# Norm sums in columns of tokens, and filler products, around the first feed-forward tiles

## The reference

```
z  = merged @ w_out
x1 = x + z * rsqrt(mean(z*z) + eps) * g_post          # first norm
h2 = x1 * rsqrt(mean(x1*x1) + eps) * g_mlp            # second norm
f  = square(relu(h2 @ w_ff1)) @ w_ff2
```

## Time and profile before

| | |
|---|---|
| median of 3 runs | 2012.83 us (2011.98 to 2015.08) |
| the profiled execution | 2014.58 us, its span 2012.8 us |
| mean granted clock of TensorE | 0.989 of full speed |
| PE busy | 1957.8 us |
| DVE, ACT, POOL busy | 903.7, 621.5, 896.5 us |

### The profile page before, as it was taken

How to read it: one execution, slowest core, us unless ns; L and a number is a source line. 1 busy time by engine, 2 the same in 40 slices (tenths; PEclk the granted TensorE clock), 3 DMA queues, 4 the chain that set the end, 5 groups by cost and what they waited for, 6 DMA issues and landing times.

```text
span 2012.8 us, 33480 instructions
## 1 busy us (share of the span) xinstructions
PE 1957.8 (97%) x13077; PEld 1908.2 (95%) x13077; DVE 903.7 (45%) x1966; ACT 621.5 (31%) x1184; POOL 896.5 (45%) x533
## 2 busy tenths in 40 slices
PE   8999999999999999999989999799999999999996
PEld 6999999999999999999969999699999999999996
DVE  6504550154403552054577743888676740111126
ACT  6312211122012220122146546644444453212121
POOL 7453233333333233423442237579777764443412
PEclk9999999999999999999999999899999999999999
DMA  5312331134211331123654354513323252223412
GB/s 190 105 43 85 136 110 43 43 115 141 74 53 58 136 136 43 43 89 141 225 175 147 123 158 129 137 46 124 124 88 125 77 211 87 103 85 105 147 53 85
DMA packets 89289, 218.22 MB, mean 108 GB/s; under 512 B 7721, under 2 KB 40745, under 8 KB 88793
## 3 DMA queue, kind: packets, MB, share of 16 engines
q1 hardware_dynamic: 78784, 192.48, 28.6%
q10 hardware_dynamic: 10392, 24.14, 3.4%
HBM read 162.93 MB, written 53.66 MB: 108 GB/s over the span
## 4 chain that ended last, share of the span: by engine, by line
PE 88%; DVE 5%; issue 2%; ACT 2%; POOL 2%; DMA 0%; DVEq 0%; SPq 0%; ACTq 0%; POOLq 0%
PE bank L892 78%; PE bank L1041 1%; PE bank L1044 1%; PE bank L1235 1%; PE bank L1033 1%; PE bank L996 1%; PE bank L1039 1%; PE bank L1133 1%; POOL w_lo L698 1%; DMA w_raw<-w_stream 0%; ACT P_sb L1437 0%; POOL h_lo L713 0%; DVE acc L2074 0%; DVE gates L2071 0%; DVE acc L1763 0%
## 5 line engine op out<-in xcount | busy, mean ns | idle before, releaser
L892 PE MATMUL bank<-h_hi,w_hi 128*128 128x344 f32 (+1 forms) x2048 | 651.1, 318 | 2.4 <-POOL w_lo L698 2.2
L892 PE MATMUL bank<-h_lo,w_hi 128*128 128x344 f32 (+1 forms) x2048 | 637.7, 311 | 0.0
L892 PE MATMUL bank<-h_hi,w_lo 128*128 128x344 f32 (+1 forms) x2048 | 636.0, 311 | 0.0
L702 POOL TENSOR_TENSOR w_hi<-w_raw,ones 128x1024 fp32r<-128x1024 f32 x77 | 147.4, 1914 | 628.1 <-PE bank L892 628.1
L892 PEld LDWEIGHTS bank<-h_hi,w_hi 128*128 128x128 f32 x2048 | 387.4, 189 | 7.1 <-issue 3.5
L892 PEld LDWEIGHTS bank<-h_hi,w_lo 128*128 128x128 f32 x2048 | 387.2, 189 | 0.9
L892 PEld LDWEIGHTS bank<-h_lo,w_hi 128*128 128x128 f32 x2048 | 387.1, 189 | 0.0
L704 POOL TENSOR_TENSOR w_lo<-w_raw,w_hi 128x1024 fp32r<-128x1024 f32 x77 | 185.7, 2412 | 6.1
L2241 DVE TENSOR_TENSOR acc<-acc,bank 128x344 f32<-128x344 f32 x72 | 36.9, 513 | 292.0 <-PE bank L892 292.0
L1268 ACT ACTIVATE side_t<-bank 128x344 f32<-128x344 f32 x96 | 44.0, 459 | 284.3 <-PE bank L892 284.3
L1763 DVE SCALAR_TENSOR_TENSOR acc<-acc,rstd 128x258 f32<-128x258 f32 x128 | 126.7, 1032 | 0.1
(11 more groups left out here) (434 smaller groups left out, 4407.7 us busy)
## 6 DMA issues: line engine op xcount, KB each, us to landing
w_raw<-w_stream SPq DMA_DIRECT2D x113, 512.0 KB, 3.7
d_side<-side_t ACTq DMA_DIRECT2D x32, 516.0 KB, 2.6
f_raw<-d_f SPq DMA_DIRECT2D x24, 516.0 KB, 4.5
gates<-d_side SPq DMA_DIRECT2D x24, 344.0 KB, 4.1
d_f<-sq SPq DMA_DIRECT2D x16, 516.0 KB, 3.3
dC<-stC SPq DMA_DIRECT2D x32, 256.0 KB, 3.7
qkb<-d_qk SPq DMA_DIRECT2D x32, 256.0 KB, 4.0
o_C_s<-dC SPq DMA_DIRECT2D x32, 256.0 KB, 2.0
```

The source lines that it names most:

```text
L702: pool.tensor_tensor(w_hi[:, slot, :], w_raw[:, slot, :], ones[:, 0:1].to_broadcast([P, 1024]), ALU.mult).then_inc(s_hi_made, 1)
L892: last = pe.matmul(out, st, mv, start=i == 0, stop=i == n - 1)
```

## The change

The four roots of the first norm and the four of the second are no longer taken over a full 128x258 tile. The squares' sum becomes the stationary operand and a single column of ones the moving one (`columns`): 3 products of 86 tokens give the sums as 86 partitions x 3 columns. Root and reciprocal work on these 86x3 elements. VectorE then spreads the reciprocals over a diagonal (86x258, `diagonal3`), and TensorE multiplies the 86x128 ones with it (`z_spread`, `x1_spread`), so that a bank has the factor in every partition again. For the second norm ScalarE copies the four results to `rstd0` (`x1_rows`). Tile 14 waits for all four copies.

The 8 squares of (1, h) are summed by 24 column products (after tile 10 for h = 0, after tile 13 for h = 1) in place of 8 full ones. `x1_sums(1)` moves behind most of the first half's `combine`; its product moves from tile 4 to tile 8. The first `combine` steps and the operands of the second half are interleaved anew on VectorE and ScalarE. Before tile 5 there are 20, before tile 7 there are 5 products of ones (`fill`) into the bank that the tile will use.

```diff
+FILLERS = {5: 20, 7: 5}
...
+            def columns(out, parts):
+                for j in range(3):
+                    for i, t in enumerate(parts):
+                        last = pe.matmul(out[0:B86, j:j + 1], t[:, B86 * j:B86 * (j + 1)], ones[:, 0:1],
+                                         start=i == 0, stop=i == len(parts) - 1)
+                return last
...
-                pe.matmul(b_mean[h][:, 0:Q4], ones[:, :], z_sum[h], start=True, stop=True).then_inc(s_z_ssq, 1)
+                columns(b_mean[h], [z_sum[h]]).then_inc(s_z_ssq, 1)
+
+            def z_spread(s, h):
+                pe.wait_ge(s_z_scaled, 18 * s + h + 1)
+                pe.matmul(b_mean[h][:, 0:Q4], ones[0:B86, :], z_std[h][0:B86, :], start=True, stop=True).then_inc(s_z_ssq, 1)
+
+            def x1_mean_first(h):
+                pe.wait_ge(s_x1_sum, 7 * (h + 1))
+                columns((bank[6], bank[3])[h], [x1_std[h]]).then_inc(s_x1_ssq, 1)
+
+            def x1_spread(s, h):
+                pe.wait_ge(s_x1_sum, 14 + 2 * s + h + 1)
+                pe.wait_ge(s_x1_std, 5 if s and h else 4)
+                pe.matmul(x1_row_bank[s][h][:, 0:Q4], ones[0:B86, :], rstd0[0:B86, qt[2 * h + s]], start=True, stop=True)\
+                    .then_inc(s_x1_ssq, 1)
...
+                if c == 17:
+                    z_spread(0, 0)
+                    z_spread(0, 1)
                 if c == 26:
-                    pe.wait_ge(s_x1_sum, 7)
-                    pe.matmul(b_mean[0][:, 0:Q4], ones[:, :], x1_std[0], start=True, stop=True).then_inc(s_x1_ssq, 1)
+                    x1_mean_first(0)
...
+            def fill(t, n):
+                copied, stepped = tile_read(tile_before(t))
+                if copied:
+                    pe.wait_ge(s_c_copied, copied)
+                if stepped:
+                    pe.wait_ge(s_c_step, stepped)
+                for _ in range(n):
+                    pe.matmul(bank[tile_bank(t)][:, 0:P], ones[:, :], ones[:, :], start=True, stop=True)
...
+                if t in FILLERS:
+                    fill(t, FILLERS[t])
...
-                    pe.wait_ge(s_x1_std, 4)
-                    pe.wait_ge(s_z_scaled, 32)
+                    pe.wait_ge(s_x1_std, 8)
+                    pe.wait_ge(s_z_scaled, 36)
...
                 elif t == 4:
-                    pe.wait_ge(s_x1_sum, 14)
-                    pe.matmul(bank[3][:, 0:Q4], ones[:, :], x1_std[1], start=True, stop=True).then_inc(s_x1_ssq, 1)
-                elif t in (6, 10):
-                    h = (t - 6) // 4
...
-                        pe.matmul(x1_mean_bank[h][:, 0:Q4], ones[:, :], x1_sq[k], start=k == 0, stop=k == 7).then_inc(s_x1_ssq, 1)
+                    z_spread(1, 0)
+                    z_spread(1, 1)
+                elif t == 8:
+                    x1_mean_first(1)
+                elif t == 10:
+                    pe.wait_ge(s_x1_ready_dve, 4)
+                    pe.wait_ge(s_xg, 24)
+                    columns(bank[6], x1_sq2).then_inc(s_x1_ssq, 1)
+                elif t == 13:
+                    pe.wait_ge(s_x1_std, 2)
+                    pe.wait_ge(s_x1_sq, 8)
+                    columns(bank[3], x1_sq).then_inc(s_x1_ssq, 1)
+                    for s in range(2):
+                        for h in range(2):
+                            x1_spread(s, h)
...
                 for k in ks:
-                    act.wait_ge(s_x1_ssq, 2 + k + 1)
+                    if k == 0:
+                        act.wait_ge(s_x1_sum, 14)
                     act.activation(x1_sq[k], x_in[:, k, qt[3]], ACT.Square).then_inc(s_x1_sq, 1)
...
+            def x1_rows(s, h):
+                act.wait_ge(s_x1_ssq, 4 + 2 * s + h + 1)
+                act.activation(rstd0[:, qt[2 * h + s]], x1_row_bank[s][h][:, 0:Q4], ACT.Copy).then_inc(s_x1_std, 1)
...
+            def diagonal3(out, col):
+                step(dve.reciprocal(col, col))
+                return dve.tensor_tensor(diag_of(out), ident[0:B86, 0:B86].unsqueeze(1).to_broadcast([B86, 3, B86]),
+                                         col.unsqueeze(2).to_broadcast([B86, 3, B86]), ALU.mult)
...
             z_inverse(1, 0)
+            z_inverse(1, 1)
             z_scale(1, 0, range(8))
-            x1_sums(1)
-            z_inverse(1, 1)
             z_scale(1, 1, range(4))
+            x1_add_last()
             b_low(0, 5)
+            combine(0, 1, "dfe", (0,))
             b_low(0, 6)
-            combine(0, 1, "dfe", (0,))
             combine(0, 2, "dfe", (0,))
-            x1_add_last()
-            for p in range(3, 7):
-                combine(0, p, "dfe", (0,))
             b_add(1, 0)
             b_add(1, 1)
+            combine(0, 3, "dfe", (0,))
             b_low(1, 0)
+            combine(0, 4, "dfe", (0,))
             b_add(1, 3)
             b_low(1, 1)
+            combine(0, 5, "dfe", (0,))
+            x1_sums(1)
             b_low(1, 2)
+            combine(0, 6, "dfe", (0,))
             b_low(1, 3)
```

More of the change, by code:

```diff
@@ L35 @@
 HEADS = 4
+B86 = 86
 L = 128
@@ L177, in hybrid_layer @@
         sm = sb("sm", [P, 16])
+        tok_col = sb("tok_col", [P, 18])
         xq_rows = sb("xq_rows", [P, 32, 32])
@@ L371, in hybrid_layer, with diag_of, z_scales @@
         x1_std = [rstd0[:, qt[2 * h]] for h in range(2)]
+        x1_sq2 = z_sq + [rstd0b[:, qt[e]] for e in range(4)]
+        z_col = [tok_col[0:B86, 3 * h:3 * h + 3] for h in range(2)]
+        x1_col = [[tok_col[0:B86, 6 + 6 * s_ + 3 * h:9 + 6 * s_ + 3 * h] for h in range(2)] for s_ in range(2)]
+        x1_row_bank = [[bank[3], bank[6]], [bank[7], bank[3]]]
+        def diag_of(t):
+            return t[0:B86, :].rearrange("p (j t) -> p j t", j=3)
+        def z_scales(s, h, k):
+            return 18 * s + 2 + 8 * h + k + 1
         f_st = [[sq0[:, 0, :], sq0[:, 1, :]], [rstd0b[:, :], zsq[:, :, :].rearrange("p g t -> p (g t)")]]
@@ L815, in x1_add @@
                 for k in ks:
-                    pool.wait_ge(s_z_scaled, 8 * (2 * s + h) + k + 1)
+                    pool.wait_ge(s_z_scaled, z_scales(s, h, k))
                     pool.tensor_tensor(x_in[:, k, q], x_in[:, k, q], acc[:, k, q], ALU.add).then_inc(s_x1_ready, 1)
@@ L1490, in root @@
                 act.wait_ge(summed, count)
-                act.activation(dst, src, ACT.Sqrt, scale=1.0 / D, bias=eps[:, 0:1]).then_inc(made, 1)
+                act.activation(dst, src, ACT.Sqrt, scale=1.0 / D, bias=eps[0:dst.shape[0], 0:1]).then_inc(made, 1)
             def z_root(s, h):
-                root(z_std[h], b_mean[h][:, 0:Q4], s_z_ssq, 2 * s + h + 1, s_z_std)
+                root(z_col[h], b_mean[h][0:B86, 0:3], s_z_ssq, 4 * s + h + 1, s_z_std)
             def wc_high(n):
@@ L1519, in x1_take @@
                         if k == 0:
-                            act.wait_ge(s_x1_sum, 14)
-                        square = x1_sq[k]
+                            act.wait_ge(s_z_ssq, 8)
+                        square = x1_sq2[k]
                     elif k == 0:
@@ L1554, in x1_root @@
             def x1_root(s, h):
[L1555 to L1558, removed]
+                root(x1_col[s][h], (bank[6], bank[3])[h][0:B86, 0:3], s_x1_ssq, 2 * s + h + 1, s_x1_std)
+            def x1_rows(s, h):
+                act.wait_ge(s_x1_ssq, 4 + 2 * s + h + 1)
+                act.activation(rstd0[:, qt[2 * h + s]], x1_row_bank[s][h][:, 0:Q4], ACT.Copy).then_inc(s_x1_std, 1)
             def b_high(s, p):
@@ L1641, in _ @@
             copy_c(0, 1, 0)
-            x1_root(0, 1)
             copy_c(0, 2, 0)
@@ L1648, in _ @@
             b_high(1, 0)
-            x1_last_square(range(4))
             b_high(1, 1)
-            x1_last_square(range(4, 8))
             wc_high(7)
             b_high(1, 2)
+            x1_last_square(range(4))
             b_high(1, 3)
+            x1_last_square(range(4, 8))
+            x1_root(0, 1)
             wc_high(8)
@@ L1659, in _ @@
             b_high(1, 6)
+            x1_root(1, 0)
             copy_c(0, 1, 1)
@@ L1663, in _ @@
             wc_high(10)
-            x1_root(1, 0)
             x1_root(1, 1)
+            for s in range(2):
+                for h in range(2):
+                    x1_rows(s, h)
             wc_high(11)
@@ L2086, in z_add @@
                    .then_inc(s_z_sum, 1)
+            def diagonal3(out, col):
+                step(dve.reciprocal(col, col))
+                return dve.tensor_tensor(diag_of(out), ident[0:B86, 0:B86].unsqueeze(1).to_broadcast([B86, 3, B86]),
+                                         col.unsqueeze(2).to_broadcast([B86, 3, B86]), ALU.mult)
             def z_inverse(s, h):
                 dve.wait_ge(s_z_std, 2 * s + h + 1)
-                step(dve.reciprocal(b_mean[h][:, 0:Q4], z_std[h]))
+                diagonal3(z_std[h], z_col[h]).then_inc(s_z_scaled, 1)
             def z_scale(s, h, ks):
                 q = qt[2 * h + s]
+                dve.wait_ge(s_z_ssq, 4 * s + 3 + h)
                 for k in ks:
@@ L2107, in x1_inverse @@
```

(17 more changed lines are left out.)

## The result

The changed kernel takes 2023.39 us (median of 5 runs, 2020.13 to 2024.77) against 2012.83 us before (5 runs): +10.6 us, ratio 1.0048 with a 95% interval of 1.0036 to 1.0060. The forecast was +2.0, within 2008.5 to 2018.8. The profiled execution took 2024.77 us, the longest of the five, and its span is 2023.0 us: 10.2 more than the span before.

A forecast was written before the change was run, and what follows sets the result against it. TensorE was taken to bound the kernel, through tile 22's start. Tile 13's end at 1323.8, plus 6.3 of chain and 11.5 of tiles, gave 1341.6 against 1339.6: +2.0 us, so 2014.8, range 2008.5 to 2018.8.

The forecast's parts named there:

- What bounds the stage: TensorE, busy 97% of the span, bounds the kernel; the change is worth only the shift of tile 22's start, 1339.6.
- First norm: Ahead of tile 5: column sums gain nothing on TensorE; VectorE's factor comes 2.3 us later; `b_low(1, 6)` ends at 1322.3.
- The 24 columns after tile 10 cost 3.4 us: After tile 10: 48 passes at 0.07 us each, 3.4 us on TensorE.
- Tile 13 at 1323.8: End of tile 13, behind its operand `b_low(1, 6)` from VectorE: 1323.8, 1.4 us earlier than before.
- Tile 14 at about 6.3: Between tiles 13 and 14: columns, root, spreads and ScalarE's last copy put tile 14 about 6.3 us after tile 13.
- 8 tiles, 11.5: Between the new chain and tile 22: TensorE's own eight tiles take 11.5 us.
- The rival that named it: New gap before tile 14: TensorE's clock falls to 0.50, costing 2.3 us: +4.3, 2017.1; chance 0.18.
- Against: no gap of the chain is over 1 us: Chain between tiles 13 and 14: argument against a falling clock, as an idle 2.9 us at 1336.7 left it full.
- The rule on the shared port: VectorE's new diagonals can be held up by POOL; once in the last chain, 0.4 us, making +2.4 of +2.0.

The follow-up runs named there:

- e9_z_full: `e5_early_full` with the first norm too over full tiles, leaving only order, places and fillers of the change: 2009.03 us, ratio 0.9979.
- e7_probe1: Kernel before plus 24 unread products with one moving column in front of each of tiles 60, 90, 120 and 150: 2036.67 us.
- e1_wide: Changed kernel with 128 moving columns of ones in place of one in all column products: 2019.80 us, ratio 1.0034.
- e4_early: Changed kernel with second-norm columns after tiles 6 and 10 (not 10 and 13), VectorE's reciprocals and diagonals right behind `b_low(1, 6)`: 2015.53 us.
- e3_full2: Changed kernel with the second norm over full tiles as in the kernel before, no spread or copies: 2011.58 us, ratio 0.9998.
- e6_early_wide: `e4_early` with 128 columns of ones as the moving operand in place of one: 2016.41 us, ratio 1.0011.
- e8_probe128: Kernel before plus 24 unread products with 128 moving columns in front of each of tiles 60, 90, 120 and 150: 2033.45 us.
- e5_early_full: `e3_full2` with its two sets of 8 full products after tiles 6 and 10 in place of 10 and 13: 2010.07 us, ratio 0.9985.

## Why the prediction was wrong

Point by point, in the order of its steps.

- **What bounds the stage**: right. Tile 22 moved by 9.8 us, from 1339.6 to 1349.4, and the span by 10.2.
- **First norm**: right. `b_low(1, 6)` was put at 1322.3 and came at 1322.1. VectorE waited 1.18 us for the spread (forecast 1 to 2) and began to scale at 1285.9 (forecast 1286.5). The 14 wide instructions took 20.1 us (13.06 + 7.07 in two windows of the trace), so 3.0 us were lost beside POOL, where I took 4.0. `e9_z_full` confirms the zero worth.
- **"The 24 columns after tile 10 cost 3.4 us"**: 3.94, and 4.71 after tile 13. The slope of the weight loads was right for the load (157 ns, forecast 154). At full clock a set takes 3.61 us (`e7_probe1`), 0.075 us a pass rather than 0.07, so 0.2 of each excess is the pass; the rest is the clock, which falls before either set has ended.
- **"Tile 13 at 1323.8"**: the failed step. It took tiles 11 to 13 at full clock behind the operands. They ran at 0.58, and tile 13 ended at 1327.0: +3.2 us. With these three tiles at full clock, 4.3 us, it would have ended at 1324.2; the last 0.4 us is the late start behind tiles 9 and 10.
- **"Tile 14 at about 6.3"**: the chain's structure was right, its clock wrong: 9.4 us, of which the columns took 1.3 more and the spreads 2.0 more than forecast. In `e1_wide`, where the clock is full, it is 8.2 with 5.25 us of wide columns in it; with the forecast 3.4 in their place it would be 6.3, with 3.61 it would be 6.5.
- **"8 tiles, 11.5"**: 13.0 us, the first two at 0.65: +1.5.

3.2 + 3.1 + 1.5 = 7.8 us; with the forecast +2.0 that is +9.8, and tile 22 moved by 9.8. Nearly the whole error is the clock; the dearer pass is 0.2 us of it in the last chain. The rival that named it priced one low stretch of 2.3 us behind tile 14 at 0.18. Its sign, a clock of 0.50 at tile 14, came. What it missed is that the clock falls *twice*, at the end of each set of 24, and that TensorE has no slack between: at half clock it, not VectorE, is the limit from tile 11 on. The sentence "Against: no gap of the chain is over 1 us" counted idle time, and counted columns as work, though the sentence before it had named them.

The rule on the shared port was right about the diagonals, more than I had allowed: by that rule, "SBUF — State Buffer", section "SBUF: two separate sides", in the Trainium skill, a VectorE instruction with two operands in SBUF and one of GpSimd lock each other out of a shared port for their whole length. The trace agrees: 1.31 us instead of 0.42 for one diagonal of the changed kernel, and for three in a row in `e4_early`. It did not decide here, since in the changed kernel POOL was idle when the last diagonals came.

**Shown:** that sets of 24 one-column products lower the clock (both probes, and `e1_wide`); that all of the loss is in the second norm's columns with their chain (`e3_full2`); that most of it comes back when the same columns stand earlier (`e4_early`); that the first norm's part and the fillers are worth nothing measurable. **Open:** how the 7.5 us of `e4_early` divide exactly between the clock and the chain's length (an estimate from the two profiles: of the 9 us by which tile 22 comes earlier, 3.6 are the set of columns that left the chain, at full clock, and much of the rest is full clock in tiles 11 to 15, at the end of that set and in the spreads); whether a chain with holes alone lowers the clock at tile 14 (`e6_early_wide`); why the better kernels gain 3.3 to 4.2 us, of which I can only point at `copy_c` and `x1_take`, which no longer wait behind `x1_root(0, 1)`, and at products that now lie in waits.

## What to carry to other kernels

Many products with one moving column in a row are cheap for TensorE in neither sense: each pays its weight load (0.157 us of load, 0.075 us from one pass to the next), and a set of 24 brought the clock down to half as idleness does. A set of 3 did no measurable harm. Before summing over partitions with such products, look at what TensorE does right behind them; if that is to be dense, a full-width product of ones may cost less in all. And work for a late factor goes into waits that are there already, not between two tiles that follow each other.

## What the runs showed of the hardware

- 48 passes of 86 weight columns and one moving column take 3.61 us at full clock (`e7_probe1`), with 128 moving columns 5.24 (`e8_probe128`, `e1_wide`).
- In a stretch without any idle time, 3.6 to 4.0 us of one-column products were followed by 2 to 6 us at 0.50 of the clock, each of four times (`e7_probe1`); 5.24 us of 128-column products by 1.00, each of four times (`e8_probe128`).
- Before tile 5 of the changed kernel, 4.5 us of real idleness read 1.00, and the tiles behind it 0.70: as with the columns, the low clock is read mostly behind what went before it.
- A VectorE instruction of 86x258 with both operands in SBUF takes 0.42 us alone and 1.3 beside POOL (changed kernel, `e4_early`); a reciprocal of 86x3 takes 0.16 (changed kernel), of 128x258 1.77 (`e5_early_full`).
